# A state-space branch computed in six parts beside a matmul stream: SyncE's turns one slab later, q and k fetched at the end of the last part, cosines made on ScalarE

## The chip, the cores and the metric

The kernel runs on one core of one Trainium2 chip. The metric is the device time of one execution in microseconds (us), the median of the runs. Five engines work side by side: TensorE (PE in the profile), VectorE (DVE), ScalarE (ACT), GpSimd (POOL) and SyncE (SP), which here does nothing but start transfers.

## The reference

Two network blocks follow each other on a sequence of 512 tokens of width 1024, all in fp32. The change lies in the first block, in its input projection and the state-space branch (S5) that is computed beside it. Cut to what matters:

```
z = rms_norm(x, g_norm) @ w_in
q, k, v, fl, gf, u, gs, qm, gm, gl = split(z)         # q, k, v, u, gs: 768 columns each
y_fox = forgetting_attention(q, k, v, log_sigmoid(fl + b_forget)) * silu(gf)
# s5_ssm(u): 48 groups of 16 channels, a complex diagonal state of 64 each
step = exp(log_step); mag = exp(lam_re * step)
ab = mag * (cos(lam_im * step), sin(lam_im * step))
h[t] = ab * h[t-1] + bb @ u[t];  y[t] = Re(C h[t]) + d * u[t]
y_s5 = gelu(y); y_s5 = y_s5 * sigmoid(y_s5 @ w_glu + b_glu) * silu(gs)
y_mem = memory_attention(qm, mk, mv) * silu(gm)
x = x + merge(y_fox, y_s5, y_mem) @ w_out
```

## The kernel before

**The stream.** The projection runs as a stream of 37 tiles (6 of u, 6 of gs, 6 of q, 6 of k, 1 of the forget gate, 12 of v), each 24 matmuls, so the stream has positions 0 to 888. The fp32 weights come in slabs of 256 columns. SyncE fetches slab i into one of three ring slots (function load_weights, L202) as soon as slab i-3 has been split. GpSimd splits each slab half by half into a high and a low part (L226 and L228); four split halves have room, so the half of positions 24j to 24j+24 can be split once the half four places ahead has been used. TensorE multiplies the split parts (L525). Slab 12 is the forget gate's, slabs 13 to 15 are v's (96 positions each), slabs 16 to 18 the GLU weights. ScalarE takes each finished tile out of one of two PSUM banks (L1026 to L1044), and stores q, k and v tiles to DRAM.

**The branch in parts.** The S5 branch is computed in six parts of 8 groups. Its small matmuls are put into the stream at fixed positions (turn_at, pad_at, out_at in the source). One part n goes like this. VectorE makes the drive table Bk (drive_table, L1364 to L1368); TensorE turns it (turn_part, L1165) and ScalarE copies it (L1216). TensorE makes the drive (L1186, signal drive_made). VectorE makes the angles (angle_table, L1377 and reduce_angle, L919 to L923); ScalarE makes sines of the angle and of the half angle (make_sines, L1222 and L1223); VectorE turns the latter into the cosine as 1 - 2 sin². ScalarE writes the drive with its halves exchanged into X (L1239, L1240), VectorE rotates it with cosine and sine and runs the scan (L1412 to L1416), makes the output table W (out_table), rotates back with the exchanged scan result, and writes the state (L1427, signal state_made). TensorE uses W for the Toeplitz part (pad_part, L1174) and, at position out_at[n], makes the output y from U and the state (L1199, L1200, signal y_made). ScalarE copies y out (L1259).

**SyncE's turns.** U, the input of a part, and y travel through DRAM, since their layout changes. SyncE does this between its slab fetches: in next_turn(n) it waits until y of part n has been made, loads U of part n+2 (8 transfers), loads y of part n-1 back, and stores y of part n (8 transfers). Everything that stands behind it in SyncE's queue waits with it. The table K.sync_turns says ahead of which slab a turn stands.

**After the stream** come six GLU tiles (L433, weights from slabs 16 to 18, VectorE's last step L1479), then y_s5 is stored and x is loaded back by ScalarE's queue (L1728), and the attention (fox) starts when q, k, v, the spread forget rows and x are there; its first instruction on VectorE is L1579.

Of the kernel before, what the change touches and what calls it, by code (L numbers as in the profile page):

```python
# [10 lines left out]
ALU = mybir.AluOpType  # L11
# [903 lines left out]
def reduce_angle(K, e, x, t):  # L915

    v = K.nc.vector
    step = lambda ins: K.link(e, "dve_step", ins)
    step(v.tensor_scalar(t, x, 1.0 / TWO_PI, ROUND, ALU.mult, ALU.add))  # L919
    step(v.tensor_scalar(t, t, ROUND, None, ALU.subtract))  # L920
    for part in (PI_1, PI_2, PI_3):
        step(v.scalar_tensor_tensor(x, t, -part, x, ALU.mult, ALU.add))
    step(v.tensor_scalar(x, x, -PI_TOP, PI_TOP, ALU.max, ALU.min))  # L923


def s5_stages(K, T):
# [151 lines left out]
    laid = K.sig("toeplitz_laid")  # L1078
# [30 lines left out]
    def next_turn(sp, n):  # L1109
        sp.wait_ge(y_made.sem, n + 1)  # L1110
        if n + 2 < PARTS:
            load_u(sp, n + 2)
        if n >= 1:
            load_y(sp, n - 1)
        store_y(sp, n)
# [13 lines left out]
    for n in range(PARTS):  # L1129
        K.sync_turns.setdefault(max(slab_at(out_at[n]) + 2, slab0 + 7), []).append(lambda sp, n=n: next_turn(sp, n))  # L1130
# [6 lines left out]
    with K.stage(before, arriving[2]) as block:  # L1137
# [67 lines left out]
        def _(e):  # L1205
# [14 lines left out]
            def make_sines(n):  # L1220
                e.wait_ge(angles.sem, n + 1)
                nc.scalar.activation(sinj[n % 2], cosj[n % 2][:, :, :], ACT.Sin).then_inc(sines.sem, 1)  # L1222
                nc.scalar.activation(half[:, :, :], half[:, :, :], ACT.Sin).then_inc(sines.sem, 1)  # L1223
# [42 lines left out]

            rest = END - out_at[-1]
# [16 lines left out]
            e.dma_start(qA[:, :, :], sq.rearrange("(t p) n -> p t n", p=P)).then_inc(qb.sem, 16)  # L1284
            e.dma_start(kA[:, :, :], sk.rearrange("(t p) n -> p t n", p=P)).then_inc(qb.sem, 16)
# [3 lines left out]
        def _(e):  # L1289
# [85 lines left out]
            def angle_table(n):  # L1375
# [3 lines left out]
                reduce_angle(K, e, x, tmp[:, :, :])  # L1379
                v.tensor_scalar(half[:, :, :], x, 0.5, None, ALU.mult).then_inc(angles.sem, 1)  # L1380
# [20 lines left out]
            for n in range(PARTS):  # L1401
# [4 lines left out]
                e.wait_ge(sines.sem, 2 * (n + 1))  # L1406
                step(v.tensor_tensor(co, half[:, :, :], half[:, :, :], ALU.mult))
                step(v.tensor_scalar(co, co, -2.0, 1.0, ALU.mult, ALU.add))
                if n + 1 < PARTS:
                    angle_table(n + 1)  # L1410
                e.wait_ge(drive_swapped.sem, n + 1)
                step(v.tensor_tensor(tmp[:, :, :], X[:, :, :], si, ALU.mult))  # L1412
# [911 lines left out]
```

## Time and profile before

| | |
|---|---|
| median of 3 runs | 2622.79 us (2621.53 to 2623.52) |
| the profiled execution | 2620.31 us, span 2618.3 us |
| PE busy | 2389.0 us, 91% of the span |
| DVE busy | 1454.3 us, 56% |
| ACT busy | 588.6 us, 22% |
| POOL busy | 1123.2 us, 43% |
| mean granted TensorE clock | 0.96 |

The profiled execution took 2.0 us more than its span and was 2.5 us below the median. Shares over the whole span say little about the branch in parts, which lies between about 132 and 323 us of the span; there each engine's idle time has to be read by itself.

### The profile page before, as it was taken

What the parts mean: (1) busy time and instruction counts of PE and PEld (TensorE: products, weight loads), DVE (VectorE), ACT (ScalarE), POOL (GpSimd) and SP (SyncE); (2) the same over time, 40 slices, a digit from 0 to 9 for tenths busy, and PEclk for the clock granted to TensorE, in tenths of its full rate; (3) what the DMA queues carried; (4) which work ended last, traced back from release to release, by engine and by line L of the source; (5) the groups of instructions that cost most, each with busy time, mean ns of one, the idle gap of its engine ahead of it and who ended that gap; (6) DMA issues with size and microseconds to landing.
All of it is one profiled execution on the core that took longest, in us unless ns stands there. A gap on an engine that the chain in (4) does not pass through costs nothing.

```text
span 2618.3 us, 30891 instructions
## 1 busy us (share of the span) xinstructions
PE 2389.0 (91%) x12709; PEld 1893.3 (72%) x12709; DVE 1454.3 (56%) x1774; ACT 588.6 (22%) x1200; POOL 1123.2 (43%) x672
## 2 busy tenths in 40 slices
PE   5788777888999969999998999998999999899998
PEld 3677645676666649987756888886997766688887
DVE  3889434433443567555457867747655436774341
ACT  2122234313222221124301433301114430100000
POOL 3524322234233344642115666673562205566663
PEclk8998888999999989999999999998999999999999
DMA  5324480342333532221122655532322104223331
GB/s 162 97 72 110 116 300 21 121 136 70 129 129 129 170 120 95 84 93 33 33 84 78 193 193 182 172 128 93 97 83 76 33 17 136 73 97 97 97 97 49
DMA packets 274280, 280.87 MB, mean 107 GB/s; under 512 B 29580, under 2 KB 256080, under 8 KB 274012
## 3 DMA queue, kind: packets, MB, share of 16 engines
q1 hardware_dynamic: 242012, 243.97, 29.4%
q10 hardware_dynamic: 32128, 34.92, 4.5%
q8 instruction: 101, 1.65, 0.3%
q14 instruction: 39, 0.32, 0.0%
HBM read 257.87 MB, written 17.85 MB: 105 GB/s over the span
## 4 chain that ended last, share of the span: by engine, by line
PE 67%; DVE 6%; ACT 1%; issue 1%; ACTq 0%; DVEq 0%
PE ps L433 43%; PE ps L1851 11%; PE ps L525 6%; PE ps L757 2%; PE ps L800 2%; PE ps L776 1%; DVE ps L864 1%; DVE normed L651 1%; DVE hT_low L641 1%; PE ps L786 1%; DVE root L646 1%; DVE ada_acc L345 1%; PE ps L627 1%; PE ps L1947 1%; PE ps L358 1%
## 5 line engine op out<-in xcount | busy, mean ns | idle before, releaser
L226 POOL TENSOR_SCALAR ring_high<-ring 128x1024 fp32r<-128x1024 f32 x302 | 337.3, 1117 | 1372.0 <-DMA ring<-in_w_in_dram 440.9
L228 POOL TENSOR_TENSOR ring_low<-ring,ring_high 128x1024 fp32r<-128x1024 f32 x302 | 757.0, 2507 | 25.2
L433 PE MATMUL ps<-hT_high,ring_high 128*128 128x512 f32 x816 | 329.2, 403 | 18.8 <-DVE hT_low L641 5.8
L433 PE MATMUL ps<-hT_low,ring_high 128*128 128x512 f32 x816 | 319.3, 391 | 0.0
L433 PE MATMUL ps<-hT_high,ring_low 128*128 128x512 f32 x816 | 319.2, 391 | 0.0
L345 DVE TENSOR_REDUCE ada_acc<-ring 128x256 f32<-128x2048 f32 x48 | 188.7, 3932 | 113.8 <-ACT ring L332 113.6
L1851 PE MATMUL ps<-ring_high,hT_high 128*128 128x256 f32 x768 | 222.5, 290 | 10.4 <-DVE hT_low L641 10.4
L1851 PE MATMUL ps<-ring_high,hT_low 128*128 128x256 f32 x768 | 220.2, 287 | 0.0
L1851 PE MATMUL ps<-ring_low,hT_high 128*128 128x256 f32 x768 | 220.2, 287 | 0.0
L332 ACT ACTIVATE ring<-ring,c_act 128x256 f32<-128x256 f32 x384 | 158.5, 497 | 187.8 <-DMA ring<-in_w_ada_dram 187.8
L433 PE MATMUL ps<-hidden_high,ring_high 128*128 128x512 f32 x512 | 200.0, 391 | 0.0
L433 PE MATMUL ps<-hidden_high,ring_low 128*128 128x512 f32 x512 | 199.3, 389 | 0.0
L433 PE MATMUL ps<-hidden_low,ring_high 128*128 128x512 f32 x512 | 199.2, 389 | 0.0
L525 PE MATMUL ps<-hT_high,ring_high 128*128 128x512 f32 x456 | 192.4, 422 | 7.0 <-DVE hT_low L639 2.5
L433 PEld LDWEIGHTS ps<-hT_high,ring_high 128*128 128x128 f32 x816 | 154.2, 189 | 59.4 <-DVE hT_low L641 11.7
L525 PE MATMUL ps<-hT_low,ring_high 128*128 128x512 f32 x456 | 181.8, 399 | 0.0
L525 PE MATMUL ps<-hT_high,ring_low 128*128 128x512 f32 x456 | 181.2, 397 | 0.0
L433 PEld LDWEIGHTS ps<-hT_low,ring_high 128*128 128x128 f32 x816 | 154.3, 189 | 32.9 <-issue 2.9
L433 PEld LDWEIGHTS ps<-hT_high,ring_low 128*128 128x128 f32 x816 | 154.0, 189 | 32.9
L2131 DVE SCALAR_TENSOR_TENSOR xT<-ps,ada,xT 128x512 f32<-128x512 f32 x64 | 48.0, 750 | 220.4 <-PE ps L433 220.3
L1851 PEld LDWEIGHTS ps<-ring_high,hT_high 128*128 128x128 f32 x768 | 150.2, 196 | 14.9 <-DVE hT_low L641 11.1
L1851 PEld LDWEIGHTS ps<-ring_high,hT_low 128*128 128x128 f32 x768 | 150.6, 196 | 0.0
(342 smaller groups left out, 4163.3 us busy)
## 6 DMA issues: line engine op xcount, KB each, us to landing
ring<-in_w_in_dram SPq DMA_DIRECT2D x75, 1024.0 KB, 5.3
ring<-in_w_ff_dram SPq DMA_DIRECT2D x64, 1024.0 KB, 5.5
ring<-in_w_ada_dram SPq DMA_DIRECT2D x48, 1024.0 KB, 7.4
ring<-in_w_out_dram SPq DMA_DIRECT2D x12, 1024.0 KB, 6.6
scratch_x<-xT ACTq DMA_DIRECT2D x3, 2048.0 KB, 7.5
xT<-scratch_x ACTq DMA_DIRECT2D x3, 2048.0 KB, 8.9
ring<-in_w_mem_kv_dram SPq DMA_DIRECT2D x4, 1024.0 KB, 5.2
ring<-in_w_branch_a_dram SPq DMA_DIRECT2D x8, 512.0 KB, 6.1
```

Source lines behind the costliest of these rows:

```text
L226: nc.gpsimd.tensor_scalar(hi, raw, 1.0, 1.0, ALU.mult, ALU.mult).then_inc(hi_done.sem, 1)
L228: nc.gpsimd.tensor_tensor(lo, raw, hi.bitcast(F32), ALU.subtract).then_inc(lo_done.sem, 1)
L332: ins = K.nc.scalar.activation(w[:, k, :], w[:, k, :], ACT.Copy, scale=K.c_act[:, k:k + 1])
L345: K.nc.vector.tensor_reduce(K.ada_acc[:, n % 2, :], K.slot(slab).rearrange("p k n -> p n k"), AX_X, ALU.add).then_inc(K.sig("ada_scaled"). ...
L358: ins = K.nc.tensor.matmul(K.ps[:, 7, 2 * (n % 2) + c:2 * (n % 2) + c + 1], K.ada_acc[:, n % 2, c * P:(c + 1) * P], K.ones[:, 0:1], start= ...
L433: ins = nc.tensor.matmul(out[0:rows, bank, cols[0]:cols[1]], lhsT, rhs, start=start, stop=stop)
L525: ins = K.nc.tensor.matmul(out, lhsT, rhs, start=start, stop=stop)
L627: nc.tensor.matmul(K.ps[:, 0, 0:n], K.ones, K.sums[:, 0:n] if summed else sq[:, k % 2, 0:n], start=(k == 0), stop=(k == KS - 1)).then_inc( ...
L757: ins = nc.tensor.matmul(s_view(i, u, w)[:, c:c + n], lhsT, rhs, start=True, stop=st["diagonal"] is None or c + n < w)
L800: ins = nc.tensor.matmul(st["place"](o_view(j), u), st["values"](u, b), turned[j % T_BUFS][:, u, b * P:(b + 1) * P], start=(b == 0), stop= ...
L1851: ins = nc.tensor.matmul(out, lhsT, rhs, start=start, stop=stop)
L2131: return v.scalar_tensor_tensor(K.xT[:, m, :], ps[:, 0, :], gate[:, m:m + 1], K.xT[:, m, :], ALU.mult, ALU.add)
```

## The change

Four things change.

1. In the table of SyncE's turns each turn stands one slab later: the turns of parts 0 to 5 stood ahead of slabs 9, 11, 12, 13, 15 and 16, and now stand ahead of slabs 10, 12, 13, 14, 16 and 16.
2. ScalarE's fetches of q and k stood behind all other work of the stage. Now they stand behind the take of the tile at out_at of the last part (position 720), after a wait for the stores of q and k. v's fetch stays at the end.
3. VectorE no longer makes the half angle (L1380), the square (L1407) and 1 - 2s² (L1408). ScalarE takes the sine of the angle with scale 0.5, squares it with scale sqrt(2) and writes 1 minus that.
4. Accordingly reduce_angle raises the signal angles_made itself, and VectorE waits for the new signal cosines_made ahead of the rotation.

```
-    step(v.tensor_scalar(x, x, -PI_TOP, PI_TOP, ALU.max, ALU.min))
+    x = v.tensor_scalar(x, x, -PI_TOP, PI_TOP, ALU.max, ALU.min)
+    if done is None:
+        step(x)
+    else:
+        x.then_inc(done.sem, 1)
...
-        K.sync_turns.setdefault(max(slab_at(out_at[n]) + 2, slab0 + 7), []).append(lambda sp, n=n: next_turn(sp, n))
+        K.sync_turns.setdefault(min(slab_at(out_at[n]) + 3, K.first["glu_z0"]), []).append(lambda sp, n=n: next_turn(sp, n))
...
-                nc.scalar.activation(half[:, :, :], half[:, :, :], ACT.Sin).then_inc(sines.sem, 1)
+                nc.scalar.activation(half[:, :, :], cosj[n % 2][:, :, :], ACT.Sin, scale=0.5).then_inc(sines.sem, 1)
+                e.wait_ge(sines.sem, 2 * n + 2)
+                K.link(e, "act_step", nc.scalar.activation(half[:, :, :], half[:, :, :], ACT.Square, scale=2.0 ** 0.5))
+                nc.scalar.activation(cosj[n % 2][:, :, :], half[:, :, :], ACT.Copy, bias=1.0, scale=-1.0
+                                     ).then_inc(cosines.sem, 1)
...
+            for x in away:
+                e.wait_ge(x.sem, 16 * 3)
+            e.dma_start(qA[:, :, :], sq.rearrange("(t p) n -> p t n", p=P)).then_inc(qb.sem, 16)
+            e.dma_start(kA[:, :, :], sk.rearrange("(t p) n -> p t n", p=P)).then_inc(qb.sem, 16)
             rest = END - out_at[-1]
...
-            e.dma_start(qA[:, :, :], sq.rearrange("(t p) n -> p t n", p=P)).then_inc(qb.sem, 16)
-            e.dma_start(kA[:, :, :], sk.rearrange("(t p) n -> p t n", p=P)).then_inc(qb.sem, 16)
             e.dma_start(vS[:, :, :], sv).then_inc(qb.sem, 16)
...
-                reduce_angle(K, e, x, tmp[:, :, :])
-                v.tensor_scalar(half[:, :, :], x, 0.5, None, ALU.mult).then_inc(angles.sem, 1)
+                reduce_angle(K, e, x, tmp[:, :, :], angles)
...
-                e.wait_ge(sines.sem, 2 * (n + 1))
-                step(v.tensor_tensor(co, half[:, :, :], half[:, :, :], ALU.mult))
-                step(v.tensor_scalar(co, co, -2.0, 1.0, ALU.mult, ALU.add))
                 if n + 1 < PARTS:
                     angle_table(n + 1)
                 e.wait_ge(drive_swapped.sem, n + 1)
+                e.wait_ge(cosines.sem, n + 1)
```

On SyncE's queue, before, from slab 6 on: three slabs, the turn of part 0 (8 loads of U, 8 stores of y), two slabs.

```order
L202 DMA ring<-in_w_in_dram 128x8x256 [waits half_split] x3
L1089 DMA U_182<-scratch_u 16x8x64 [waits y_made]
L1089 DMA U_182<-scratch_u 16x8x64 x7
L1095 DMA scratch_y<-Y 16x8x64 [waits y_copied]
L1095 DMA scratch_y<-Y 16x8x64 x7
L202 DMA ring<-in_w_in_dram 128x8x256 [waits half_split] x2
```

Now, at the same place:

```order
L202 DMA ring<-in_w_in_dram 128x8x256 [waits half_split] x4
L1093 DMA U_182<-scratch_u 16x8x64 [waits y_made]
L1093 DMA U_182<-scratch_u 16x8x64 x7
L1099 DMA scratch_y<-Y 16x8x64 [waits y_copied]
L1099 DMA scratch_y<-Y 16x8x64 x7
L202 DMA ring<-in_w_in_dram 128x8x256 [waits half_split] x2
```

Slab 9 has moved ahead of the first turn. Behind that the groups of slabs between the turns keep their sizes (2, 1, 1, 2) but each holds slabs one number higher: slab 13, which stood behind the turn of part 3, now stands behind that of part 2. The last group (slab 15 alone, between the turns of parts 4 and 5) is gone.

On ScalarE, at the sines of part 1 (cosj_174 holds the angles, xT the sines), before:

```order
L1216 ACTIVATE BkT<-ps 128x1024 [waits drive_made,bk_turned]
L1038 ACTIVATE staged<-ps 128x512 [waits stream_made]
L1054 DMA scratch_q<-staged 128x512 [waits stream_taken]
L1222 ACTIVATE xT<-cosj_174 128x512 [waits angles_made]
L1223 ACTIVATE half_angle<-half_angle 128x512
L1239 ACTIVATE swapped<-scanned 64x512 [waits scan_made]
L1240 ACTIVATE swapped<-scanned 64x512
```

Now:

```order
L1220 ACTIVATE BkT<-ps 128x1024 [waits drive_made,bk_turned]
L1042 ACTIVATE staged<-ps 128x512 [waits stream_made]
L1058 DMA scratch_q<-staged 128x512 [waits stream_taken]
L1226 ACTIVATE xT<-cosj_174 128x512 [waits angles_made]
L1227 ACTIVATE half_angle<-cosj_174 128x512
L1229 ACTIVATE half_angle<-half_angle 128x512 [waits sines_made]
L1230 ACTIVATE cosj_174<-half_angle 128x512 [waits act_step]
L1247 ACTIVATE swapped<-scanned 64x512 [waits scan_made]
L1248 ACTIVATE swapped<-scanned 64x512
```

Two instructions stand between the sines and the exchange of the scan's result that VectorE waits for, and no table load is among them.

On ScalarE, behind y of the last part, now:

```order
L1267 ACTIVATE Y<-ps 128x512 [waits y_out0,y_made]
L1048 ACTIVATE staged<-ps 128x256 [waits qkv_away3,qkv_away2,stream_made]
L1277 DMA qA<-scratch_q 128x6x512 [waits qkv_away2,qkv_away3,qkv_away1,qkv_away0]
L1278 DMA kA<-scratch_k 128x6x512
L1048 ACTIVATE staged<-ps 128x256 [waits stream_made]
```

Before, the two fetches stood after ten further takes and GELUs of this stage, directly ahead of that of v.

## Rows read from the trace of the kernel before

**Rows 1.** Waits of PE, 60 to 420 us: total, times, longest, us.

```profile
PE ps L1174 <- DVE W L1368: 13.2, 2, 7.2
```

**Rows 2.** Timeline of ACT, ScalarE's copies of y, one per part: start, duration.

```profile
178.35 0.60 ACT L1259 ACTIVATE Y<-ps 128x512 f32<-128x512 f32 x1 [13.06 <-PE ps L1200]
...
201.71 0.60 ACT L1259 ACTIVATE Y<-ps 128x512 f32<-128x512 f32 x1 [8.28 <-PE ps L1200]
...
236.13 0.60 ACT L1259 ACTIVATE Y<-ps 128x512 f32<-128x512 f32 x1 [15.24 <-PE ps L1200]
...
263.86 0.60 ACT L1259 ACTIVATE Y<-ps 128x512 f32<-128x512 f32 x1 [7.71 <-PE ps L1200]
...
302.84 0.60 ACT L1259 ACTIVATE Y<-ps 128x512 f32<-128x512 f32 x1 [9.50 <-PE ps L1200]
...
323.08 0.60 ACT L1259 ACTIVATE Y<-ps 128x512 f32<-128x512 f32 x1 [8.76 <-PE ps L1200]
```

**Rows 3.** Windows of PE: length, busy (instructions), PEclk, DMA share, GB/s.

```profile
178.35:201.70 23.35, 23.35 (x140) 1.00 0.64 170
...
167.60:173.00 5.40, 5.40 (x21) 0.54 0.00 0
...
233.00:245.00 12.00, 12.00 (x51) 0.57 0.35 84
288.10:292.00 3.90, 3.90 (x18) 0.50 0.00 0
```

**Rows 4.** SyncE's queue behind part 3's turn; PE at position 600 (timelines).

```profile
274.19 1.34 SPq L202 DMA_DIRECT2D ring<-in_w_in_dram  x2
...
288.09 0.55 PE L525 MATMUL ps<-ring_high,hT_high 128*128 128x256 f32 x1 [13.32 <-POOL ring_low L228]
```

**Rows 5.** Timeline of POOL, first and last row of four halves in a row.

```profile
193.95 1.04 POOL L226 TENSOR_SCALAR ring_high<-ring 128x1024 fp32r<-128x1024 f32 x1 [34.19 <-DMA ring<-in_w_in_dram]
...
209.10 2.70 POOL L228 TENSOR_TENSOR ring_low<-ring,ring_high 128x1024 fp32r<-128x1024 f32 x1
```

**Rows 6.** Timeline of DVE: part 1's rotations and state, tables of parts 2 and 3.

```profile
169.96 1.22 DVE L1364 TENSOR_TENSOR Bk<-pow_re,B 128x1024 f32<-128x1024 f32 x1
...
173.62 0.68 DVE L1407 TENSOR_TENSOR cosj<-half_angle 128x512 f32<-128x512 f32 x1
174.34 0.43 DVE L1408 TENSOR_SCALAR cosj<-cosj 128x512 f32<-128x512 f32 x1
...
175.99 0.43 DVE L920 TENSOR_SCALAR rotated<-rotated 128x512 f32<-128x512 f32 x1
...
181.36 0.69 DVE L1412 TENSOR_TENSOR rotated<-swapped,xT 128x512 f32<-128x512 f32 x1 [1.84 <-ACT swapped L1240]
...
193.27 0.69 DVE L1423 TENSOR_TENSOR rotated<-swapped,xT 128x512 f32<-128x512 f32 x1 [3.26 <-ACT swapped L1240]
194.01 1.51 DVE L1427 TENSOR_TENSOR state<-cosj,rotated 128x504 f32<-128x504 f32 x1
...
212.12 0.43 DVE L920 TENSOR_SCALAR rotated<-rotated 128x512 f32<-128x512 f32 x1
```

**Rows 7.** Groups of ACT, 128 to 324 us: count, busy us, mean ns, idle before.

```profile
L1223 ACT ACTIVATE half_angle<-half_angle 128x512 f32<-128x512 f32 x6 | 3.7, 615 | 0.0
```

**Rows 8.** Timeline of ACT, the take of the forget tile.

```profile
278.54 0.68 ACT L1033 ACTIVATE xT<-ps,b_forget_col 12x512 f32<-12x512 f32 x1
```

**Rows 9.** DMA issues, 300 to 420 us: count, KB each, us to landing.

```profile
ring<-in_w_glu_dram SPq DMA_DIRECT2D x3, 768.0 KB, 10.2
...
kA<-scratch_k ACTq DMA_DIRECT2D x1, 1536.0 KB, 14.2
```

**Rows 10.** Timelines after the last part: SyncE's queue, PE, DVE.

```profile
329.90 2.13 SPq L202 DMA_DIRECT2D ring<-in_w_glu_dram  x3
...
343.09 2.31 PE L433 MATMUL ps<-yP,ring 128*128 128x512 f32 x5
...
396.34 0.23 DVE L1579 CAST causal_half<-causal 128x128 bf16<-128x128 f32 x1 [15.00 <-DMA xT<-scratch_x]
```

More of the change, by code:

```diff
@@ L912, in exact_exp, with reduce_angle @@
     step(v.scalar_tensor_tensor(out, p, 1.0, t, ALU.add, ALU.mult))
-def reduce_angle(K, e, x, t):
+def reduce_angle(K, e, x, t, done=None):
     v = K.nc.vector
@@ L1077, in s5_stages @@
         "bkT_copied", "toeplitz_copied", "sines_made", "drive_swapped", "scan_swapped", "y_copied"))
-    laid = K.sig("toeplitz_laid")
+    laid, cosines = K.sig("toeplitz_laid"), K.sig("cosines_made")
     sm, ln, fr, qb, gelu = (K.sig(s) for s in ("forget_summed", "forget_ln", "forget_rows", "fox_loaded", "y_gelu"))
```

## The prediction

> **What bounds the kernel now.** First I read the page: TensorE is busy for 91% of the span. The change touches only the branch in parts, about 132 to 323 us, and the fetches behind it, so I asked for TensorE's waits up to 420 us. In the branch it stops mainly at three places: twice for VectorE's output table W, 13.2 us in all, the longer 7.2 and so the other 6.0 [rows 1], and once, at stream position 600, for GpSimd's split of slab 13, 13.32 us [rows 4]. Then I read ScalarE's copies of y, which mark the end of each part: 178.35, 201.71, 236.13, 263.86, 302.84, 323.08 [rows 2]. The intervals are 23.36, 34.42, 27.73, 38.98 and 20.24. In the first TensorE was busy throughout at a granted clock of 1.00 [rows 3]: 23.4 us is TensorE's own work for such a part. The reader is to see that the next two intervals exceed that by 15.4 us together. Last came the clock in the windows: behind the waits it is granted at about half for a while, 0.54 in 5.4 us, 0.57 in 12 us, 0.50 in 3.9 us [rows 3]. A window of length L at clock c loses L(1-c): 2.5, 5.2 and 1.9 us.
>
> All terms below are of this stage, and what comes later starts when it ends, so I count them one to one.
>
> **A: slab 13 (SyncE's turns).** Before, slab 13 stands behind part 3's turn, which waits for y at 263.86; the turn's issues take until 274.19, 10.3 us [rows 2, 4]. TensorE resumes at 288.09, so it stopped at 274.77 [rows 4]. After the change slab 13 stands behind part 2's turn, a whole part (over 23 us) earlier, and lands before GpSimd may split it. Its second half can then be split when position 576 has been used: between there and 600 lie 24 stream matmuls and a turn, more than the 3.7 us (1.04 + 2.70) of a split [rows 5]. The whole 13.3 go, and the slow restart of 1.9. What is late next is the PSUM bank of the forget tile, which TensorE wants again at position 624. ScalarE takes that tile by 279.2, 15.4 us after part 3's y [rows 2, 8], and 1.3 later by edit C: 16.7. TensorE stopped 10.9 us after that y, and the next 24 matmuls are narrow ones, some 3 us by the spacing in a full stretch: it comes at 14, and waits 2.7. A = -13.3 - 1.9 + 2.7 = **-12.5 us**. Ends: -9, if the takes cost twice that and the clock falls again, and -15.2, if they cost nothing.
>
> The other slabs: slab 14 stands behind part 3's turn as before and is wanted 96 positions later than slab 13; slab 15 no longer waits for part 4's y. Part n+2's U and the y round trips wait for the same y as before, and the earlier slabs ahead of them are gated by splits long done, so they move with the parts. Parts 4 and 5 now turn together ahead of slab 16, but the later was the last to end there before too.
>
> **B and C: VectorE loses three instructions per part.** By the spacing of their starts (173.62 to 174.34, and one of the 0.43 kind with its gap, twice) they are 0.72 + 0.46 + 0.46 = 1.64 us per part where nothing disturbs [rows 6].
>
> How much this is worth depends on GpSimd. From the drive table of part 2 (169.96) to the second angle instruction (175.99) VectorE took 6.0 us; the same instructions of part 3, from the state's end (195.5) to 212.12, took 16.6 [rows 6], and beside them GpSimd split four halves without a pause [rows 5]. So one split costs VectorE (16.6 - 6.0)/4 = 2.65 us. The four came together since slabs 9 and 10 waited for part 0's y. After the change slab 9 is there early, and splits come two to a part, when a half is freed. This does not lower their number, only their bunching.
>
> B, the first wait for W (6.0 us, then 2.5 lost to the clock): the wait follows VectorE's chain of part 0, in which two splits stand. Shorter by 1.64 undisturbed; one of the removed instructions stood against a split there, for which I add some 1.9. Wait -3.5; the remaining 2.5 us is half as long as the waits after which the clock fell, so I take most of that too: B = **-5.8 us** (ends -1.6 and -8.5).
>
> C, parts 1 to 3. VectorE's own time for a part: from 169.96 to the state's end at 195.52, less its waits of 1.84 and 3.26 for ScalarE, is 20.5 us [rows 6]. Less 1.64, plus 0.7 for the skip's addition (sized as L1412) is 19.5; plus two splits, 5.3, is 24.8. TensorE needs 23.4. So VectorE stays just ahead as the bound: three parts in 74.4 us instead of 85.5 [rows 2], C = **-11.1 us**. The 5.2 us of slow clock around 236 are in that. Ends: -15.4 (TensorE bound) and -3 (see the second rival).
>
> What ScalarE gains in work: square and copy, 2 x 0.62 us [rows 7] and a short wait between them, about 1.3 us, right ahead of the exchange of the scan's result. In part 1 VectorE waited for exactly that, 3.26 us, and will wait longer. The state was ready at 195.5, 6.2 us before y's copy at 201.71 [rows 2, 6]; y's 32 matmuls fit in 5.3 even at the mean of that window (23.35 us for 140), so at least 0.9 us of cover was there, probably more. If the cover is gone, at most 0.4 us per part: nothing in the sum, 1.5 in the range.
>
> VectorE and GpSimd in the Trainium skill, SBUF — State Buffer, section Who interferes with whom: the port pair that both use is an exclusive lock held for a whole instruction, and an operation with two SBUF inputs contends with GpSimd's reads. By that rule each split would cost VectorE all of its 3.7 us, not 2.65, and C would be 3 x 2 x 1.05 = 6.3 us less. The rows show less, and the sum goes by them.
>
> **D: q and k fetched earlier.** They land long before they are needed in both kernels: the attention starts at 396.34, after 15.00 us of waiting for x, which is fetched behind y_s5's last step [rows 10]. q, k and v were still landing (kA 14.2 us [rows 9]) while a slab of the next stage was fetched; that slab's split comes sooner, its successor is fetched sooner, and x then shares the DMA engines with less. I take **-2 us** (0 to -5).
>
> What they collide with instead: y of part 5 and the GLU weights. The weights were issued at 329.90, 6.8 us after the last y, and land 10.2 later, 17.0; TensorE wants the first at 343.09, 20.0 after [rows 2, 9, 10], and 10.2 is the median of three. Cover 3 us for the median one, more for the first. I take no cost.
>
> **Sum.** -12.5 - 5.8 - 11.1 - 2 = -31.4. The profiled execution took 2620.3, so 2588.9; the median of the runs stood 2.5 above it: 2591.4, forecast **2591 us**. The time of each case below is on the median's scale.
>
> **Rivals.**
> 1. Likeliest, as summed, chance 0.60: 2581 to 2600.
> 2. VectorE stays fully bound. Splits, spread out, each meet it in full at 3.7: C shrinks by 6.3 to -4.8, B to -3.5, the rest stays: -22.8, 2600. The 16.6 us stretch speaks for it in kind, its size against. 0.16, 2596 to 2604. The rule of SBUF — State Buffer in the Trainium skill, above, gives this case.
> 3. Only slab 13's wait goes, ScalarE's 1.3 us per part and the splits eat the rest: A -12.5, B -1.6, C 0: 2609. 0.12, 2604 to 2614.
> 4. q and k get in the way: if the DMA engines served them first, 14.2 us [rows 9], y's store and the GLU weights behind it would be late by up to that less 3 us of cover: 11 us, 2602. Against it: small transfers landed between large ones all through the stage. The Trainium skill, DMA: Bandwidth & Descriptors, section Queues, rings and completion order, says that each engine takes turns between queues packet by packet, by which the weights would be a few us late at most. 0.06.
> 5. Slower. ScalarE becomes the bound of all five parts that have a successor: what the two instructions with their waits add, x us, costs x minus its cover (0.9 to about 3) in each. To turn -31 into +5 it has to be about 9 us per part; at 10 with 2 of cover that is +40, 2631. The 0.62 each [rows 7] speak against it, a table load between them would not do, and none is there. 0.03.
> 6. No change that can be measured, within 2617.5 and 2628: slab 14 becomes what slab 13 was, and A is only moved: 0.03. It is wanted 96 positions later.
>
> Faster, same and slower by more than 0.2% (5.2 us, about what a measurement of this kernel can tell from no change) are 0.94, 0.03 and 0.03. The range that leaves out about 2 in 10 is 2580 to 2608.
>
> **What the profile after would show.** A: no wait of L525 for ring_low near position 600, a short one for ScalarE instead. B: the first wait of L1174 down to 2 to 3 us. C: y copies 24 to 26 us apart in parts 1 to 3, GpSimd's splits in pairs, no clock near half in 12 us together. D: qA and kA issued about 1 us after the last Y, L433 starting 20 us after it without a wait, L1579's wait for x 13 us or so. ScalarE: square and copy at about 0.62 us each. The prediction is wrong if the waits for W remain as long, if TensorE waits for the state (L1199) in several parts, or if L433 waits for the GLU weights.

## The result, and the profile after

The median after is 2605.02 us (four runs, 2601.70 to 2608.21), and 2623.15 us for the kernel before in the same rounds (four runs, 2621.53 to 2626.76). The ratio is 0.9931, 95% interval 0.9914 to 0.9947: 18 us faster, where 31 were forecast. The profiled execution took 2601.70 us with a span of 2599.7; against the span before, 2618.3, that is 18.6 us.

The ends of the parts come first, ScalarE's copies of y in its timeline (start, duration, what it waited for). They answer to [rows 2].

```profile
174.41 0.60 ACT L1267 ACTIVATE Y<-ps 128x512 f32<-128x512 f32 x1 [12.39 <-PE ps L1204]
198.27 0.60 ACT L1267 ACTIVATE Y<-ps 128x512 f32<-128x512 f32 x1 [7.51 <-PE ps L1204]
228.27 0.60 ACT L1267 ACTIVATE Y<-ps 128x512 f32<-128x512 f32 x1 [13.14 <-PE ps L1204]
254.71 0.60 ACT L1267 ACTIVATE Y<-ps 128x512 f32<-128x512 f32 x1 [7.71 <-PE ps L1204]
283.87 0.60 ACT L1267 ACTIVATE Y<-ps 128x512 f32<-128x512 f32 x1 [11.55 <-PE ps L1204]
304.17 0.60 ACT L1267 ACTIVATE Y<-ps 128x512 f32<-128x512 f32 x1 [9.08 <-PE ps L1204]
```

The intervals are 23.86, 30.00, 26.44, 29.16 and 20.30; before they were 23.36, 34.42, 27.73, 38.98 and 20.24. The last y comes 18.9 us earlier, as much as the span lost. Of it 1.0 is chance ahead of the branch: the first turn starts at 131.12, before at 132.09, and between 130.46 and 132.72 in the experiments. The rest are the terms. The changed kernel was profiled a second time (e12 below), and the last column has that profile, since single profiles differ by a few us:

| term | forecast | measured in the profiles | the second profile (e12) |
|---|---|---|---|
| B, from the first turn's start to the first y | -5.8 | 46.26 to 43.29: -3.0 | 41.59: -4.7 |
| C, the next three y | -11.1 | 85.51 to 80.30: -5.2 | 81.03: -4.5 |
| A, part 4's interval | -12.5 | 38.98 to 29.16: -9.8 | 27.35: -11.6 |
| D, last y to the attention's first cast | -2 | 73.26 to 74.29: +1.0 | 72.87: -0.4 |
| sum | -31.4 | -17.0 | -21.2 |

TensorE's waits by line and releaser, 60 to 420 us (total, times, longest), say what is left:

```profile
PE ps L1178 <- DVE W L1378: 7.3, 2, 4.5
PE ps L776 <- ACT fox_turned L832: 6.2, 6, 2.1
PE ps L525 <- ACT staged L1042: 5.3, 3, 2.8
PE ps L525 <- ACT staged L1048: 4.9, 1, 4.9
PE ps L525 <- ACT xT L1037: 1.7, 1, 1.7
PE ps L757 <- ACT fox_probs L819: 1.7, 1, 1.7
PE ps L433 <- DMA ring<-in_w_glu_dram: 1.4, 1, 1.4
PE ps L1203 <- DVE state L1434: 0.3, 1, 0.3
```

TensorE's wait for GpSimd at position 600 [rows 4] is gone. The waits for the table W fell from 13.2 [rows 1] to 7.3. The waits of the stream (L525) for a PSUM bank (the memory that TensorE writes) that ScalarE has not yet emptied grew: L1042 and L1037, 7.0 us together, where the same copies cost 1.5 before. The 4.9 us for L1048 lie in part 5 and were 5.2 before. TensorE's timeline has their places (start, duration, in brackets the wait):

```profile
164.45 3.46 PE L1178 MATMUL ps<-W,B 128*16 128x128 f32 x16 [2.83 <-DVE W L1378]
...
217.72 3.59 PE L1178 MATMUL ps<-W,B 128*16 128x128 f32 x16 [4.46 <-DVE W L1378]
...
240.62 0.50 PE L525 MATMUL ps<-hT_high,ring_high 128*128 128x512 f32 x1 [2.81 <-ACT staged L1042]
...
267.22 0.39 PE L525 MATMUL ps<-ring_high,hT_high 128*128 128x256 f32 x1 [1.60 <-ACT staged L1042]
...
272.10 0.38 PE L525 MATMUL ps<-ring_high,hT_high 128*128 128x256 f32 x1 [1.75 <-ACT xT L1037]
...
294.87 0.58 PE L525 MATMUL ps<-ring_high,hT_high 128*128 128x256 f32 x1 [4.89 <-ACT staged L1048]
```

Windows at three of those places (length, busy time and instructions of PE, PEld, DVE, ACT, POOL, then the granted clock, DMA share, GB/s) show the slow clock in and behind them:

```profile
164.00:168.00 4.00, 3.55 (x17) 2.38 (x18) 3.88 (x7) 0.00 (x0) 0.00 (x0) 0.57 0.00 0
216.00:220.00 4.00, 2.29 (x11) 1.62 (x12) 3.88 (x6) 0.00 (x0) 0.45 (x1) 0.50 0.17 64
220.00:224.00 4.00, 4.00 (x17) 2.88 (x15) 3.93 (x5) 0.00 (x0) 0.00 (x0) 0.72 0.00 0
272.00:276.00 4.00, 3.90 (x22) 2.81 (x22) 3.95 (x4) 0.32 (x2) 3.92 (x3) 0.68 0.51 180
```

The second profile (e12) does not have it everywhere. Behind its waits of 2.63 and 1.75 us at the first and the last of these places the clock was granted in full, and behind that of 4.46 it was not:

```profile
164.00:168.00 4.00, 3.94 (x25) 3.22 (x26) 3.85 (x8) 0.00 (x0) 0.27 (x1) 1.00 0.00 0
216.00:220.00 4.00, 3.76 (x17) 2.48 (x18) 3.88 (x8) 0.00 (x0) 0.00 (x0) 0.50 0.01 3
...
274.00:278.00 4.00, 4.00 (x37) 4.00 (x35) 0.00 (x0) 0.00 (x0) 3.92 (x3) 1.00 0.01 4
```

### The profile page after: what moved, and what is told of

The parts are those of the page before. It is cut to its first block, busy times and chain, and to the rows that moved or that the text cites. A ratio compares the mean times of both kernels' runs of the same rounds, so it can differ in the third digit from the quotient of the medians.

```text
span 2599.7 us, 30892 instructions
## 1 busy us (share of the span) xinstructions
PE 2384.8 (92%) x12709; PEld 1889.6 (73%) x12709; DVE 1454.2 (56%) x1756; ACT 597.2 (23%) x1212; POOL 1126.4 (43%) x672
## 4 chain that ended last, share of the span: by engine, by line
PE 68%; DVE 5%; ACT 1%; issue 1%; ACTq 0%; DVEq 0%
PE ps L433 43%; PE ps L1858 11%; PE ps L525 6%; PE ps L757 2%; PE ps L800 2%; PE ps L776 1%; DVE ps L864 1%; DVE normed L651 1%; DVE hT_low L641 1%; PE ps L786 1%; DVE root L646 1%; PE ps L627 1%; PE ps L1954 1%; PE ps L358 0%; DVE squares_summed L585 0%
## 5 line engine op out<-in xcount | busy, mean ns | idle before, releaser
L433 PE MATMUL ps<-hT_high,ring_high 128*128 128x512 f32 x816 | 329.1, 403 | 19.1 <-DVE hT_low L641 5.8
L433 PE MATMUL ps<-hT_low,ring_high 128*128 128x512 f32 x816 | 319.3, 391 | 0.0
L433 PE MATMUL ps<-hT_high,ring_low 128*128 128x512 f32 x816 | 319.2, 391 | 0.0
L433 PE MATMUL ps<-hidden_high,ring_high 128*128 128x512 f32 x512 | 200.0, 391 | 0.0
L525 PE MATMUL ps<-hT_high,ring_high 128*128 128x512 f32 x456 | 191.5, 420 | 9.2 <-ACT staged L1042 3.7
L433 PE MATMUL ps<-hidden_high,ring_low 128*128 128x512 f32 x512 | 199.3, 389 | 0.0
L433 PE MATMUL ps<-hidden_low,ring_high 128*128 128x512 f32 x512 | 199.2, 389 | 0.0
L433 PEld LDWEIGHTS ps<-hT_high,ring_high 128*128 128x128 f32 x816 | 154.3, 189 | 59.8 <-DVE hT_low L641 11.7
L525 PE MATMUL ps<-hT_low,ring_high 128*128 128x512 f32 x456 | 180.9, 397 | 0.0
L525 PE MATMUL ps<-hT_high,ring_low 128*128 128x512 f32 x456 | 180.8, 396 | 0.0
L433 PEld LDWEIGHTS ps<-hT_low,ring_high 128*128 128x128 f32 x816 | 154.3, 189 | 32.9 <-issue 2.9
L433 PEld LDWEIGHTS ps<-hT_high,ring_low 128*128 128x128 f32 x816 | 154.0, 189 | 32.6
L1858 PEld LDWEIGHTS ps<-ring_high,hT_high 128*128 128x128 f32 x768 | 149.6, 195 | 14.7 <-DVE hT_low L641 11.1
```

The costliest lines, as they stand in the source:

```text
L433: ins = nc.tensor.matmul(out[0:rows, bank, cols[0]:cols[1]], lhsT, rhs, start=start, stop=stop)
L525: ins = K.nc.tensor.matmul(out, lhsT, rhs, start=start, stop=stop)
L1858: ins = nc.tensor.matmul(out, lhsT, rhs, start=start, stop=stop)
```

## The experiments

Twelve kernels ran in three groups, each with five rounds. The medians of the kernel before in the groups were 2622.3, 2622.3 and 2623.1 us. "Intervals" are those between y copies; the first number is from the first turn's start to the first y, which for the changed kernel is 43.29. The edits are shortened here to what they change.

### Each part of the change undone

**e1: the turns back.**

```diff
-min(slab_at(out_at[n]) + 3, K.first["glu_z0"])
+max(slab_at(out_at[n]) + 2, slab0 + 7)
```

> The changed kernel with SyncE's turns put back one slab earlier; q and k early and the cosines on ScalarE stay. By the intervals between ScalarE's copies of y the slab-13 wait gave 9.8 us (38.98 to 29.16) and the earlier slab 9 shares in the 5.2 us won over parts 1 to 3. Theory (the turns carry most of the change): 10 to 14 us slower than the changed kernel, about 2616, with a wait of L525 for ring_low near 13 us back in the trace. Rival (the waits are linked, and VectorE's shorter chain would have hidden part of them anyway): under 8 us slower.

2619.35 us, ratio 0.9986 (0.9973 to 0.9998). Intervals 43.32; 23.80, 32.94, 27.97, 41.08, 19.21. TensorE waits 14.49 us for `ring_low` again. So without the turns little of the gain is left, and the turns are worth 14 to 15 us. The first y does not move (43.32 against 43.29): B owes nothing to them.

**e2: half angle, square and cosine back on VectorE.**

```diff
-activation(half, cosj, ACT.Sin, scale=0.5); activation(half, half, ACT.Square, scale=2.0 ** 0.5)
-activation(cosj, half, ACT.Copy, bias=1.0, scale=-1.0)
+v.tensor_scalar(half, x, 0.5, None, ALU.mult); activation(half, half, ACT.Sin)
+v.tensor_tensor(co, half, half, ALU.mult); v.tensor_scalar(co, co, -2.0, 1.0, ALU.mult, ALU.add)
```

> The changed kernel with the half angle, the square and the cosine back on VectorE; turns and q and k stay as changed. Theory 1 (VectorE with GpSimd's splits is the bound of parts 0 to 3): each part is longer by 1.64 us plus what a tensor_scalar that meets a split loses, up to 2.1: 7 to 10 us slower than the changed kernel, and the waits of L1178 for W grow from 7.3 to over 12 us. Theory 2 (ScalarE's chain, 1.3 us longer per part with the change, is the bound since the turns moved): within 3 us of the changed kernel, either way.

2605.56 us, ratio 0.9929 (0.9911 to 0.9947), as with the change. Intervals 45.33; 23.71, 31.58, 28.06, 25.68, 19.20. The waits for W are 10.9 us (4.36 and 6.51). So the cosines on ScalarE win 2.0 us up to the first y and 1.6 in each of the parts 2 and 3, about what VectorE's three instructions take (1.64), and part 4, which is 3.5 us shorter without them, gives most of it back. Single profiles scatter by as much, but the first number holds in all of them: 41.6 to 44.4 in the eleven with the cosines on ScalarE, 45.3 to 46.3 in the three with them on VectorE (before, e2, e10). Part 4 took 27.35 in the second profile of the changed kernel, 1.7 more than here.

**e3: q and k fetched where they were.**

```diff
-dma_start(qA, sq), dma_start(kA, sk) right behind the last copy of y
+dma_start(qA, sq), dma_start(kA, sk) just ahead of dma_start(vS, sv)
```

> The changed kernel with q and k fetched at the end of the stage again, ahead of v. In the changed kernel y of part 5 came back 7 us later against the last y than before, and TensorE waited 1.44 us for the GLU weights; x was waited for as long as before (15.1 us). Theory 1 (the early fetch costs its collision and wins nothing at the attention's start): 1 to 2 us faster than the changed kernel, L433 without a wait for its weights. Theory 2 (as predicted, the early fetch frees the DMA engines for x): 1 to 3 us slower.

2605.86 us, ratio 0.9928 (0.9907 to 0.9949). Last y to cast 72.52 us, wait for x 14.87 (15.12 with the change, 15.00 before [rows 10]), and the wait for the GLU weights (L433) is gone. The medians differ by 0.8 us and decide nothing. Nor does the time from the last y to the cast: 72.5 to 74.5 us in the profiles with the early fetch, 72.5, 73.3 and 74.5 in the three without (e3, before, e11). No gain of the early fetch can be seen.

### Where the turns gain

**e9: one turn alone.** Turns ahead of slabs 9, 11, 12, **14**, 15 and 16 instead of 9, 11, 12, **13**, 15 and 16.

```diff
-K.sync_turns.setdefault(min(slab_at(out_at[n]) + 3, K.first["glu_z0"]), [])
+K.sync_turns.setdefault(slab0 + (9, 11, 12, 14, 15, 16)[n], [])
```

> The changed kernel with SyncE's turns where the kernel before has them, except that of part 3, which stands ahead of slab 14 instead of 13; so of the turns only slab 13's place is changed. The theory that slab 13 carries most of the turns' gain: the interval between the y copies of parts 3 and 4 falls from the 41.1 us of the run with all turns back to about 29, those of parts 1 to 3 stay as there (23.8, 32.9, 28.0), and the kernel takes about 2608. The rival, that moving the first turns is what matters and slab 13's wait only shows up because the rest is late: the interval stays at 35 or more and the time at 2614 or more.

2607.55 us, ratio 0.9941 (0.9928 to 0.9953). The copies of y in its ScalarE timeline start at 175.23, 199.20, 232.32, 260.16, 290.96 and 310.07: intervals 43.30; 23.97, 33.12, 27.84, 30.80, 19.11. Part 4 falls by 10.3 us against e1 and the first three intervals stand still. One entry of the table carries 11.8 us by the medians (2619.35 - 2607.55), of the 18 in all; it moves slab 13 out from behind a turn that waits for y. The other turns are worth 2.5 to 3.4 us by the medians; in the profiles most of that lies in part 2 (33.12 against 30.00).

**e4: all turns later still**, ahead of slabs 12, 13, 14, 15, 16 and 16.

```diff
-K.sync_turns.setdefault(min(slab_at(out_at[n]) + 3, K.first["glu_z0"]), [])
+K.sync_turns.setdefault(slab0 + (12, 13, 14, 15, 16, 16)[n], [])
```

> The changed kernel with the turns of parts 0 to 5 ahead of slabs 12, 13, 14, 15, 16 and 16 (was 10, 12, 13, 14, 16, 16), so that slabs 10 and 11 no longer wait for y of part 0. Theory 1 (four splits met VectorE in part 2 because slab 10 landed late, at 190 us; that is why the part took 30.0 us): its splits spread to two per part, the 4.5 us wait for W and the slow clock behind it go, the interval falls to about 25, 4 to 6 us faster than the changed kernel. Theory 2 (ScalarE's tile takes are next in line): the wait moves to L525 for staged tiles, at most 2 us faster. Theory 3 (a split costs VectorE the same wherever it stands): nothing.

2603.51 us, ratio 0.9919 (0.9899 to 0.9939). Intervals 44.19; 23.33, 29.19, 26.04, 29.10, 20.05, and the wait of 4.46 us for W is there to the hundredth. GpSimd's halves begin at 187.19, 194.63, 205.55 and 211.81 instead of 190.02, 194.28, 205.74 and 211.99. How closely the fetches let the splits follow one another was not what is left.

### What is left: VectorE beside the splits

**e5: most of the low part left out** for ten halves.

```diff
+if 18 <= j < 28:  # slabs 9 to 13
+    nc.gpsimd.tensor_tensor(lo[:, 0:1, 0:16], raw[:, 0:1, 0:16], hi[:, 0:1, 0:16], ALU.subtract)
+else:
     nc.gpsimd.tensor_tensor(lo, raw, hi.bitcast(F32), ALU.subtract)
```

> The changed kernel, where GpSimd forms the low part of weight halves 18 to 27 (slabs 9 to 13) for 16 columns of one block only; so the low parts of these five slabs are left out and everything else stands. The theory that VectorE and the splits beside it bound part 2 of the branch: each split that is gone gives VectorE back about 2.6 us, four lie between the y copies at 198.27 and 228.27, so that interval falls from 30.0 to about 24, TensorE's wait for W of 4.5 us at 217.7 goes, and the kernel takes about 2597 to 2599. The rival, that ScalarE's tile takes and transfers' issues hold that part: the interval stays within 1.5 us of 30 and the time within 2 us of 2605. In both the waits of part 3 and 4 for ScalarE's bank copies stay at about 2.8 and 1.6 us.

2597.1 us, ratio 0.9900 (0.9883 to 0.9918). Copies of y at 173.75, 197.09, 220.42, 246.59, 273.76 and 293.64: part 2 takes 23.33 instead of 30.00, which is what part 1 takes, TensorE's own time. The wait for W at 217 is gone. (Four splits meet VectorE between the ends of its tables W of parts 1 and 2, at 187.83 and 217.66 us; between the two y copies, where the expectation put them, only two begin.)

VectorE's chain from part 2's drive table (`Bk`, first row) to the end of its output table (`W`, last row) shows the price of one split. Timeline of the changed kernel:

```profile
194.32 2.08 DVE L1374 TENSOR_TENSOR Bk<-pow_re,B 128x1024 f32<-128x1024 f32 x1
196.43 3.25 DVE L1376 TENSOR_TENSOR t<-pow_im,B 128x1024 f32<-128x1024 f32 x1
...
207.35 3.30 DVE L1423 TENSOR_TENSOR_SCAN scanned<-rho,rotated 128x512 f32<-128x512 f32 x1
...
214.28 3.38 DVE L1378 TENSOR_TENSOR W<-W,t 128x1152 f32<-128x1152 f32 x1
```

Timeline of e5, the same instructions:

```profile
191.44 1.22 DVE L1378 TENSOR_TENSOR Bk<-pow_re,B 128x1024 f32<-128x1024 f32 x1
192.70 1.23 DVE L1380 TENSOR_TENSOR t<-pow_im,B 128x1024 f32<-128x1024 f32 x1
...
202.28 1.22 DVE L1427 TENSOR_TENSOR_SCAN scanned<-rho,rotated 128x512 f32<-128x512 f32 x1
...
207.05 1.36 DVE L1382 TENSOR_TENSOR W<-W,t 128x1152 f32<-128x1152 f32 x1
```

217.66 - 194.32 = 23.34 us against 208.41 - 191.44 = 16.97. The reader is to see that the surplus sits in single instructions, 3.25 against 1.23, 3.30 against 1.22, 3.38 against 1.36: 2.0 to 2.1 us whenever a subtraction of GpSimd stands beside one. Three subtractions fall in this stretch, 6.1 of the 6.4 us; the rest is one more copy of the high part, three here and two in e5's. A copy cost VectorE up to 0.9 us (2.08 against 1.22 in the first row). GpSimd's timeline of the changed kernel has them, and in its last row, from later in the kernel, a subtraction beside which VectorE did nothing:

```profile
194.28 1.05 POOL L226 TENSOR_SCALAR ring_high<-ring 128x1024 fp32r<-128x1024 f32 x1 [0.42 <-PE ps L525]
195.41 3.19 POOL L228 TENSOR_TENSOR ring_low<-ring,ring_high 128x1024 fp32r<-128x1024 f32 x1
205.74 1.05 POOL L226 TENSOR_SCALAR ring_high<-ring 128x1024 fp32r<-128x1024 f32 x1 [7.13 <-PE ps L525]
206.87 2.70 POOL L228 TENSOR_TENSOR ring_low<-ring,ring_high 128x1024 fp32r<-128x1024 f32 x1
211.99 1.05 POOL L226 TENSOR_SCALAR ring_high<-ring 128x1024 fp32r<-128x1024 f32 x1 [2.42 <-PE ps L525]
213.13 3.32 POOL L228 TENSOR_TENSOR ring_low<-ring,ring_high 128x1024 fp32r<-128x1024 f32 x1
...
366.93 2.34 POOL L228 TENSOR_TENSOR ring_low<-ring,ring_high 128x1024 fp32r<-128x1024 f32 x1
```

Alone a subtraction takes 2.34 us. Beside VectorE it takes 0.4 to 1.0 us more, so GpSimd loses too: the one at 206.87 is recorded 0.45 us before VectorE ends L1421 at 207.32, and lasts 0.36 us longer than alone.

### What is left: ScalarE behind its own transfers

**e6: ScalarE takes the stream's tile between the Toeplitz transfers**, not behind all eight, and the forget tile ahead of part 5's sines.

```diff
 for r in range(CH):
+    if r == 4 and n + 1 < PARTS:
+        stream.take(e, turn_at[n + 1])
     e.dma_start(TT5[...
 ...
     copy_turned(n + 1)
+    if n + 1 == PARTS - 1:
+        stream.take(e, 600)
     make_sines(n + 1)
```

> The changed kernel, with ScalarE's tile take moved in between the fourth and the fifth of the eight Toeplitz transfers that it issues in a row, and one F-tile take of the last part ahead of its sines. The theory that these issues keep ScalarE from handing TensorE's banks back: the waits for its staged copies (0.8, 2.8, 1.6 us) and for xT (1.75 us) go, 4 to 6 us in all, and the kernel takes about 2600. The rival, that VectorE bounds the parts whatever ScalarE does: the waits move to W and the state and the time stays within 1.5 us of 2605. A third: the late half of the transfers delays the Toeplitz tiles, the y copies come later, and the time is 2607 or more.

2599.53 us, ratio 0.9910 (0.9891 to 0.9928). Intervals 42.88; 23.34, 30.20, 24.80, 23.69, 18.95. The bank waits of 0.84, 2.81, 1.60 and 1.75 us are gone, as TensorE's waits from 60 to 420 us show:

```profile
PE ps L1178 <- DVE W L1382: 9.1, 3, 4.5
PE ps L776 <- ACT fox_turned L832: 7.2, 7, 2.2
PE ps L525 <- ACT staged L1048: 4.9, 1, 4.9
```

The one of 4.9 us in part 5 stays. It has the same cause, eight issues in a row (287.93 to 293.10 us in the changed kernel) ahead of the copy that TensorE waits for; the edit leaves that row as it is, and no run moved it.

Why they stood there, ScalarE's timeline of the changed kernel shows, here in part 3; an ACTq row is the time for issuing transfers:

```profile
231.28 1.02 ACT L1237 ACTIVATE pad<-ps 16x1024 f32<-16x1024 f32 x1
232.33 6.63 ACTq L1244 DMA_DIRECT2D TT<-pad  x8
239.06 1.02 ACT L1220 ACTIVATE BkT<-ps 128x1024 f32<-128x1024 f32 x1 [6.76 <-issue]
239.98 0.59 ACT L1042 ACTIVATE staged<-ps 128x512 f32<-128x512 f32 x1
```

The copy that TensorE waits for until 240.62 stands behind eight issues of 0.83 us each. With the take between them it runs at 234.02. The profiled execution of e6 was its fastest (2593.89 us); the medians differ by 5.5 us from the first timing of the changed kernel and by 4.6 from its second (e12), as forecast, but the intervals of the ratios overlap, so this size is likely and not settled. The branch itself, from the first turn to the last y, took 163.9 us here and 166.7 in e11, which has the same edit, against 173.1 and 169.7 in the two profiles of the changed kernel.

**e10: e6 with the cosines back on VectorE** (the edit of e2 on top).

> The run with the tile take between the Toeplitz transfers and the early F-tile take (2599.5 us), with half angles, squares and cosines back on VectorE. The theory that the cosines on ScalarE pay as soon as ScalarE is not the one that is late: the parts bound by VectorE grow by what those operations take there, the intervals from part 1's y on rise by 1 to 2 us each and the kernel takes 2604 to 2606. The rival, that the place of that work matters in neither version: 2599.5 within 1.5 us.

2604.80 us, ratio 0.9929 (0.9915 to 0.9942). Intervals 45.59; 23.34, 31.86, 24.00, 30.85, 20.86; the waits for W are 15.2 us in four places (5.23, 6.39, 0.55, 3.03). That is 5.3 us more than e6 and 3.4 more than e11, which ran in the same group; the intervals of the ratios overlap here too. The branch decides more clearly: 176.5 us against 163.9 (e6) and 166.7 (e11). So the cosines on ScalarE pay once ScalarE's copies are not late. In the changed kernel that gain and ScalarE's lateness nearly cancel (173.1 and 169.7 us with, 173.6 without), which is why e2 showed none.

**e8: cosines on VectorE in part 5 alone**, with the turns of e4.

```diff
+if n == PARTS - 1: return            # ScalarE: no square, no copy for part 5
+if n + 1 == PARTS:                   # VectorE: the two operations of before
+    step(v.tensor_tensor(co, half, half, ALU.mult))
+    step(v.tensor_scalar(co, co, -2.0, 1.0, ALU.mult, ALU.add))
```

> SyncE's turns ahead of slabs 12, 13, 14, 15, 16 and 16, and the cosines on ScalarE for parts 0 to 4 but on VectorE for part 5, with the two operations of the kernel before. The theory that ScalarE is the one that is late around part 5 (its copies keep TensorE 1.75 and 1.6 us) and VectorE in the parts before: the last interval but one falls from 29.1 to about 26, the first four stay, and the time is 2600 to 2601. The rival, that the gain of the interval measured without cosines on ScalarE came from where the parts stood against the slabs: the interval stays at 29 and the time at 2603.5.

2601.43 us, ratio 0.9915 (0.9897 to 0.9933). Intervals 43.37; 23.34, 30.26, 26.10, 26.03, 20.45. Part 4 falls from 29.10 to the 26 that was expected, and its wait for the forget tile from 1.76 to 0.43. The two waits there save 1.4 us; the rest is the clock behind them, granted at 0.64 from 272 to 276 us in e4 and at 1.00 here. The medians, 2603.51 and 2601.43, do not tell the two apart by themselves.

**e7: e6 with the turns of e4.**

> As the last one, with SyncE's turns ahead of slabs 12, 13, 14, 15, 16 and 16 as well. If both gains are apart they add: 2598 to 2600. If the later turns and the earlier takes work on the same wait, the time is that of the better one alone, about 2603.

2604.89 us, ratio 0.9928 (0.9911 to 0.9944): a miss for both, neither 2599 nor 2603. Intervals 43.30; 23.34, 30.32, 24.76, 27.87, 20.23. The bank waits are gone here too, but TensorE waits 2.51 us for W at 271.44, which e6 does not. The traces show why: with the turns of e4 a split begins at 265.50 us, beside the last two instructions of part 4's table W, which take 2.08 and 3.41 us instead of the 1.36 each of e6, where the next split begins at 268.63, behind the table.

**e11: e6 with q and k fetched where they were.**

> The same run with q and k fetched where the kernel before fetches them. Both theories of the early fetch tell something small: if it only delays y's store and the GLU weights, this is up to 1.5 us faster, 2598 to 2599.5, and TensorE's wait for the GLU weights (1.6 us) goes; if it relieves the start of the attention, this is slower, 2601 or more.

2601.38 us, ratio 0.9914 (0.9900 to 0.9927), within the scatter of e6; the wait for the GLU weights is gone. TensorE waits 1.70 us for W in part 4, which takes 25.48 instead of 23.69: two executions of the same branch differ by that much. The place of that fetch does not matter there either.

**e12: the changed kernel again.**

> The changed kernel unaltered, to compare the variants with it in the same rounds: 2605 within 2 us.

2604.11 us, ratio 0.9920 (0.9906 to 0.9933). Intervals 41.59; 24.31, 30.31, 26.41, 27.35, 19.72. The same waits stand at the same places (4.46 for W, 2.76, 1.40 and 1.75 for banks), but there is none for the GLU weights, and the clock was not low behind all of them. Its last y is 3.6 us earlier than in the first profile and its span 4.0 longer, so stages that the change does not touch scatter by 7.6 us between two executions of one program. A gain of a few microseconds has to be read in the stage where it arises. That stage, from the start of the first turn to the last copy of y, took in the one profile of each run:

| run | median, us | the branch, us |
|---|---|---|
| before | 2623.15 | 191.0 |
| changed kernel, and again (e12) | 2605.02, 2604.11 | 173.1, 169.7 |
| e1, all turns back | 2619.35 | 188.3 |
| e2, cosines back | 2605.56 | 173.6 |
| e3, q and k back | 2605.86 | 175.6 |
| e4, turns later | 2603.51 | 171.9 |
| e5, low parts left out | 2597.10 | 163.0 |
| e6, banks earlier | 2599.53 | 163.9 |
| e7, e6 and e4 | 2604.89 | 169.8 |
| e8, e4 and part 5's cosines back | 2601.43 | 169.6 |
| e9, one turn | 2607.55 | 178.1 |
| e10, e6 and e2 | 2604.80 | 176.5 |
| e11, e6 and e3 | 2601.38 | 166.7 |

## Why the forecast held, and where it was off

Faster, and inside the range of 2580 to 2608, near its upper end; each of A, B and C had its sign, and the sum was almost twice what came, 31.4 us against 17.0 in the profiles and 18 by the medians. By its steps:

**A, slab 13: right in mechanism, 2.7 us too much.** The wait of 13.3 us and the whole of it go by one entry of the table (e9). The next thing late was named, the forget tile's bank. It was sized at 2.7; TensorE waited 1.60 for the tile before it and 1.75 for it, 3.35 together, and behind that the clock was granted at 0.68, for which the sum had nothing. The low clock was partly chance: in e12 it was 1.00 behind the same waits, and part 4 took 27.35, 0.9 us more than forecast (38.98 - 12.5 = 26.5). Without both, part 4 takes 23.69 (e6) or 25.48 (e11), so they cost 2 to 5.5 us.

**B, the first wait for W: its cause right, 2.8 too much.** The wait was to fall by 3.5 and fell by 3.2, from 6.0 to 2.83, through the cosines alone (e1 has it, e2 has not). The step that came out only in part is "I take most of that too". From W's matmuls to the first y it took 10.76 us before (167.59 to 178.35) and 9.96 now (164.45 to 174.41), 0.8 less where 2.3 were forecast: the granted clock behind the shorter wait was 0.57. In e12, behind a wait of 2.63, it was 1.00 and the same stretch took 8.42. Two executions of one program differ here, so the forecast could not tell which it would meet. The other 1.4 us lie at the branch's start, where the forecast had nothing: from the first turn to part 0's first matmuls with W TensorE took 10.59 us before (132.09 to 142.68) and 11.97 now (131.12 to 143.09), with the clock at 0.63 in 132 to 136 us before and at 0.50 now. In all experiments it took 11.3 to 12.0. Why the one profile of the kernel before had less is open. A bank wait at 157 us takes 0.84 here and took 1.24 before.

**C, parts 1 to 3: here the sum failed, by 5.9 us.** The step is "splits come two to a part", in the sum 5.3 us per part. A part spans 66 positions of the stream and a half 24, so 2.75 splits come to a part: GpSimd made eight between the y copies at 174.41 and 254.71, not six, as its groups of that stretch show (count, busy us, mean ns):

```profile
L228 POOL TENSOR_TENSOR ring_low<-ring,ring_high 128x1024 fp32r<-128x1024 f32 x8 | 24.6, 3073 | 0.7
```

By the forecast's own numbers 19.5 + 2.75 x 2.65 = 26.8 us per part, 80.4 for three; 80.30 were measured. The price of a split, 2.65 us, was about right: e5 finds 2.0 to 2.1 for the subtraction, and a copy costs 0.7 to 0.9 more. That the sum comes out so closely is luck, for it is not spread evenly. Between the ends of its tables W, VectorE met two splits in part 1, four in part 2 and two in part 3. Part 1 ran at TensorE's pace (23.86), part 2 was VectorE's and took 30.0, and 2.81 of part 3's 26.4 are the bank wait; only in part 2 did TensorE wait for W. VectorE's own time was less than 19.5 too, 18.6 by e5: 23.23 us from part 3's drive table to part 4's, less a wait of 3.77 and 0.84 beside a copy. The part from which the forecast took it had such a copy beside its state (1.51 us [rows 6], alone 0.67). The cover for ScalarE's added work held for the state (L1203 waits 0.3 us in all); the forecast did not look at the other thing that queues behind that work and the transfers, the stream's tile.

**D, q and k: no gain.** The forecast had 2 us; the wait for x, which was to shrink to 13, is what it was, 15.12 us. Rival 4 was partly right: SyncE's queue reads part 5's y back 12.97 us after the last copy of y, where in e3 it is 5.98 (312.07 - 306.09), and only then issues the GLU weights:

```profile
305.02 4.42 SPq L1099 DMA_DIRECT2D scratch_y<-Y  x8
317.14 0.34 SPq L1105 DMA_DIRECT2D yP<-scratch_y  x1
...
318.00 2.92 SPq L202 DMA_DIRECT2D ring<-in_w_glu_dram  x3
```

Their 13.8 us after y instead of 6.8 [rows 10] used up the cover, and TensorE waited 1.4 us for them, which the forecast had named as a sign of being wrong. The second profile (e12) does not have that wait, and the +1.0 at the attention's start is within the scatter of that time (e3). The DMA queues from 304 to 318 us (packets, MB, share of the engines) show ScalarE's q10 with q and k beside SyncE's q1 with the y stores:

```profile
q10 hardware_dynamic: 2066, 3.65, 73.6%
q1 hardware_dynamic: 1440, 0.79, 20.5%
...
scratch_y<-Y SPq DMA_DIRECT2D x8, 32.0 KB, 7.4
```

A store took 7.4 us to land, in e3 1.8. The Trainium skill, DMA: Bandwidth & Descriptors, section Queues, rings and completion order, has the engines take turns by packet. The rows do not contradict it, but they do not show the order of turns. By the profile's count q10's packets hold 1.8 KB on average (3.65 MB / 2066) and q1's 0.55 (0.79 / 1440); if turns are equal, a queue of small packets gets fewer bytes than the large transfer beside it, an argument that no run tested. I had taken the rule to mean that small transfers get through.

**The rivals.** The measured 2605.0 lies outside the range of the likeliest case (2581 to 2600) and inside that of rival 3 (2604 to 2614); the nearest single time is rival 4's 2602: its delay of the GLU weights came, 7 us of it, but cost TensorE 1.4. Rival 3, only slab 13's wait, is right in that this wait is most of the gain: e9, which moves nothing else in SyncE's turns, took 84.9 us for parts 1 to 3, 0.6 less than before. But with all turns C was 5.2, not 0. Rival 2, VectorE bound with each split at its full 3.7 us, had B and C at -3.5 and -4.8, close to the -3.0 and -5.2 that came. That is luck: two splits at 3.7 are 7.4 us, and 2.75 at 2.65 are 7.3. It was the number of splits that was larger, not their price.

The Trainium skill, SBUF — State Buffer, section Who interferes with whom, calls the port pair that VectorE and GpSimd share an exclusive lock. The traces of the changed kernel and e5 agree: a VectorE instruction beside a subtraction grows by 2.0 to 2.1 us, most of the 2.34 that the subtraction takes alone, and the subtraction by 0.4 to 1.0. The 3.7 us that the forecast took for a split by this rule (1.04 + 2.70) are recorded times beside VectorE, with GpSimd's own waiting in them.

Rivals 5 and 6 did not come. The changed kernel did show the sign of rival 5 in part 4, where e2 is 1.7 to 3.5 us shorter.

## What to carry to other kernels

Find the one fetch that stands in its queue behind a wait for a later result; moving it is worth the stall, here 12 of 18 us with one number of a table. When an engine's load is counted per part, count the disturbances in the same unit as the parts, here positions of the stream: 66/24, not "two". When work moves to an idle engine, look at everything in its queue that someone waits for, PSUM copies above all, and keep such copies out from behind a row of transfer issues; then the move pays (e6 and e11 against e10), and else it nearly cancels itself (e2). Profile the same kernel twice before explaining a few us.

## What the runs showed of the hardware

- Eight transfers issued in a row keep ScalarE 5.2 to 6.8 us, 0.65 to 0.85 each, although it does no arithmetic; four take 2.6 to 4.3 (all runs).
- A subtraction of GpSimd over 128x1024 fp32 takes 2.34 us alone and 2.7 to 3.4 beside VectorE, and the VectorE instruction beside it grows by 2.0 to 2.1 (3.25 against 1.23). A copy of 1.05 us costs VectorE 0.7 to 0.9 (changed kernel and e5).
- Around TensorE's waits of 2.83 and 4.46 us the granted clock was 0.57 (164 to 168 us) and 0.50, then 0.72 (216 to 220 and 220 to 224): near its lower level of 1.2 GHz, though the waits before had been 6.0 and 7.2 us. In a second execution of the same program it was 1.00 behind a wait of 2.63 us at the first of these places, and the stretch to the first y took 8.42 us instead of 9.96.
- Two executions of one program differed by 7.6 us between the last part's end and the end of the kernel.
